# Cached values on TensorE: two batches of four pages in a row every fourth tick, in place of one batch every second tick

## The reference

```python
def diff_attn_sample(q, k_new, v_new, k_past, v_past, lam):
    ...
    s = jnp.concatenate([s_past, jnp.where(causal, s_new, -jnp.inf)], axis=-1)
    p = jax.nn.softmax(s, axis=-1)
    a = (p[:, :, 0] - lam * p[:, :, 1]).astype(v_new.dtype)
    return (jnp.einsum('bhqk,bkhv->bqhv', a[..., :P], v_past)
            + jnp.einsum('bhqk,bkhv->bqhv', a[..., P:], v_new))
```

## Time and profile before

| | us |
|---|---|
| median of 3 timed runs (lowest, highest) | 1393.79 (1392.96, 1394.21) |
| profiled execution, its own time | 1391.86 |
| its span in the profile | 1390.1 |
| PE busy in the span | 1352.7 (97%) |
| DVE / ACT / POOL busy | 900.0 / 579.4 / 397.4 |
| first and last value matmul start (line 3353) | 712.5 and 958.4 |

### The profile page before, as it was taken

One profiled execution on the slowest core, in us unless ns is written; L12 is line 12 of the kernel. 1 busy time (PEld: TensorE's weight loads), 2 busy tenths in 40 slices (PEclk: granted clock), 3 DMA queues, 4 the chain that ended last, 5 costly groups with the idle time before them and its releaser, 6 DMA issues.

```text
span 1390.1 us, 23920 instructions
## 1 busy us (share of the span) xinstructions
PE 1352.7 (97%) x8605; PEld 1124.6 (81%) x8605; DVE 900.0 (65%) x1619; ACT 579.4 (42%) x1075; POOL 397.4 (29%) x395
## 2 busy tenths in 40 slices
PE   9998999999999999999999999999999999999998
PEld 7777877776777767777767766667999999999998
DVE  6479668845648877647657565525376666887785
ACT  7463333315546554623224241314344543435432
POOL 3547424525523544243000000000152102322130
PEclk9999999999999999999999999999999999999999
DMA  9458634434254564577476575874454654232201
GB/s 325 114 183 238 215 136 132 156 118 130 90 159 160 192 231 133 175 253 243 130 267 223 189 250 175 291 229 169 163 193 153 213 204 148 74 122 107 107 32 62
DMA packets 125544, 239.30 MB, mean 172 GB/s; under 512 B 13601, under 2 KB 46658, under 8 KB 125426
## 3 DMA queue, kind: packets, MB, share of 16 engines
q1 hardware_dynamic: 116226, 213.64, 46.4%
q10 hardware_dynamic: 9200, 24.13, 5.2%
HBM read 197.64 MB, written 40.09 MB: 171 GB/s over the span
## 4 chain that ended last, share of the span: by engine, by line
PE 63%; DVE 6%; ACT 2%; issue 2%; DMA 1%; POOL 1%; SPq 1%; ACTq 0%; DVEq 0%; POOLq 0%
PE ps L87 18%; PE ps L89 17%; PE ps L88 17%; PE ps L3353 2%; PE ps L1548 2%; PE ps L1585 1%; PE ps L1367 1%; DMA kr<-in_cache_k 1%; DVE uw_l L2071 1%; ACT uw_h L2065 1%; PE ps L1569 1%; DVE sd L3107 1%; DVE dl L2164 1%; PE ps L1781 1%; DMA vr<-in_cache_v 0%
## 5 line engine op out<-in xcount | busy, mean ns | idle before, releaser
L3118 POOL TENSOR_TENSOR kr<-kr,qb 128x512 f32<-128x512 f32 x128 | 170.6, 1342 | 168.8 <-DMA kr<-in_cache_k 167.6
L87 PE MATMUL ps<-x2hB,uw_h 128*128 128x264 f32 (+1 forms) x512 | 145.2, 284 | 0.7 <-DVE x2lB L2906 0.7
L88 PE MATMUL ps<-x2lB,uw_h 128*128 128x264 f32 (+1 forms) x512 | 144.7, 283 | 0.0
L89 PE MATMUL ps<-x2hB,uw_l 128*128 128x264 f32 (+1 forms) x512 | 144.5, 282 | 0.0
L87 PE MATMUL ps<-part_h,fh 128*128 128x264 f32 (+1 forms) x448 | 127.8, 285 | 0.0
L89 PE MATMUL ps<-part_h,fl 128*128 128x264 f32 (+1 forms) x448 | 127.0, 284 | 0.0
L88 PE MATMUL ps<-part_l,fh 128*128 128x264 f32 (+1 forms) x448 | 126.9, 283 | 0.0
L87 PE MATMUL ps<-uh,dh 128*128 128x512 f32 x256 | 105.8, 413 | 7.2 <-DVE dl L2164 4.9
L2891 DVE TENSOR_TENSOR xt<-xt,ps 128x264 f32<-128x264 f32 (+1 forms) x224 | 87.3, 421 | 35.8 <-PE ps L89 35.6
L3107 DVE TENSOR_REDUCE sd<-kr 128x8 f32<-128x512 f32 x128 | 84.9, 675 | 35.0 <-POOL kr L3118 34.9
L87 PE MATMUL ps<-x2hA,uw_h 128*128 128x512 f32 x256 | 105.6, 412 | 0.0
(11 more groups left out here) (392 smaller groups left out, 3430.3 us busy)
## 6 DMA issues: line engine op xcount, KB each, us to landing
kr<-in_cache_k SPq DMA_DIRECT2D x128, 256.0 KB, 3.4
raw_up<-in_w_up_units SPq DMA_DIRECT2D x64, 512.0 KB, 4.7
vr<-in_cache_v SPq DMA_DIRECT2D x128, 256.0 KB, 3.5
raw_dn<-in_w_down SPq DMA_DIRECT2D x32, 512.0 KB, 6.5
raw_dn<-in_w_down ACTq DMA_DIRECT2D x32, 512.0 KB, 4.9
raw<-in_w_in_units SPq DMA_DIRECT2D x23, 512.0 KB, 6.2
raw_up<-in_w_out_units SPq DMA_DIRECT2D x16, 512.0 KB, 4.3
kept_up_low<-uw_l SPq DMA_DIRECT2D x14, 512.0 KB, 6.6
```

What stands on the lines that cost most here:

```text
L87: pe.matmul(out, lh, rh, start=first and n == 0, stop=False, skip_group_check=onto)
L88: pe.matmul(out, lh, rl, start=False, stop=False, skip_group_check=onto)
L89: ins = pe.matmul(out, ll, rh, start=False, stop=last and n == len(ks) - 1, skip_group_check=onto)
L3118: pool.tensor_tensor(k[:, :], k[:, :], qb[v // PAGES][:, :], ALU.mult).then_inc(k_multiplied, 1)
```

## The change

The body that issues a batch becomes a function, `unit(u)`. The tensor stream calls it for two batches, u - 1 and u, at the tick of each odd batch u, and no more at the ticks of the even ones. The ticks of `total`, of ACT's copies, of DVE's adds and of SP's loads are as they were. SP's waits name the same semaphore values.

```diff
+        def unit(u):
+            b, l = divmod(u, 4)
+            pe.wait_ge(v_in[u % VRING], keys_in[u % VRING] + 64 * (u // VRING + 1))
...
+            if l == 0 and b >= 2:
+                pe.wait_ge(v_added, b)
+            for g in range(4):
+                ins = pe.matmul(ps[32 * g:32 * g + 32, 2 + b % 2, :], sd[:, b, 4 * l:4 * l + 4, :].rearrange("p g h -> p (g h)"),
+                                vring[(4 * u + g) % 8][:, :], start=l == 0, stop=l == 3, tile_position=(0, 32 * g))
+            ins.then_inc(v_used, 1)
+
         for s in range(STEPS):
             u, j = divmod(s - 3, 2)
-            if j == 0 and 0 <= u < VALUE_UNITS:
-                b, l = divmod(u, 4)
-                pe.wait_ge(v_in[u % VRING], keys_in[u % VRING] + 64 * (u // VRING + 1))
...
-                ins.then_inc(v_used, 1)
+            if j == 0 and u % 2 and 0 <= u < VALUE_UNITS:
+                unit(u - 1)
+                unit(u)
             b, j = divmod(s - 11, 8)
             if j == 0 and 0 <= b < NS:
                 total(b)
```

More of the change, by code:

```diff
@@ L3340, in total @@
             ins.then_inc(v_totalled, 1)
+        def unit(u):
+            b, l = divmod(u, 4)
+            pe.wait_ge(v_in[u % VRING], keys_in[u % VRING] + 64 * (u // VRING + 1))
+            if u == 0:
+                pe.wait_ge(sem("exp_made"), 4)
+                pe.wait_ge(sem("coef_made"), 1)
+            if l == 0 and b >= 2:
[4 more added lines that the diff above has]
+            ins.then_inc(v_used, 1)
         for s in range(STEPS):
             u, j = divmod(s - 3, 2)
-            if j == 0 and 0 <= u < VALUE_UNITS:
-                b, l = divmod(u, 4)
-                pe.wait_ge(v_in[u % VRING], keys_in[u % VRING] + 64 * (u // VRING + 1))
[L3347 to L3354, removed]
-                ins.then_inc(v_used, 1)
+            if j == 0 and u % 2 and 0 <= u < VALUE_UNITS:
+                unit(u - 1)
+                unit(u)
             b, j = divmod(s - 11, 8)
```

## The result

| | before | after | ratio (95% interval) |
|---|---|---|---|
| median, us (first comparison) | 1393.26 | 1402.21 (1399.59 to 1404.78) | 1.0059 (1.0046 to 1.0072) |
| median, us (second comparison) | 1394.14 | 1402.71 (1399.33 to 1407.60) | 1.0065 (1.0043 to 1.0087) |
| span of the profiled execution | 1390.1 | 1400.5 | |

The forecast was 1393.9 us, with 1390.7 to 1398.2 as its range. The time lies above the range.

What follows compares the result with a forecast made beforehand. PE, busy 97% of the span, was taken as the bound. Terms -2.9 (stretches), -0.7 (old wait), +0.6 and +0.4 (DVE), +2.7 (page waits) sum to +0.1 us: 1393.9 us forecast, range 1390.7 to 1398.2.

Steps and rivals of the forecast that it cites:

- The stretches: On PE, nine stretches in the batches' matmul shape go, seven stay for `total`; 0.32 us each, 2.9 us saved.
- The check that I named for it: In the profile after, "issue" idle time in front of the value line falls from 10.2 to about 6 us.
- VectorE's stop: Around 830, PE waits 2.6 instead of 1.4 us for DVE's `dl`; moving batch 14 costs 0.32 instead of saving it: +0.64.
- The +0.4 for batch 6: With batch 6 moved, PE reaches the next tiles 1.2 us earlier than DVE's `dl` allows and waits about 0.4 us.
- The page waits: Second batches of pairs (22,23) and (24,25) wait 1.4 and 1.25 us for pages, +2.7 together; thirteen other intervals within 0.3.
- A sign that I had named for being wrong: The prediction is wrong if pairs before 867 wait for pages, a weight load comes late, or the two waits are missing.
- the walk: Fifteen intervals between pairs checked for late page loads, using SP's order and times; called right to about half a microsecond per tight place.
- The two waits that were named: DMA waits inside the pairs at 901 and 914, (22,23) and (24,25): 1.4 and 1.25 us, each over 1 us.
- Rival 2: Serial issue on SP becomes the bound, second batches late first from 867 on; +3.5 to +4.5, time 1398.3 us, chance 0.16.
- Rival 3: A stop of PE lowers its clock; fifteen slow dense intervals are 3.0 us, time 1396.9 us, chance 0.06.
- "Total follows as before": ACT's copy of a finished sequence waits for its fourth, odd batch, and `total` follows as before; no cost was given.
- Loads behind the value loads priced at nothing: Weights, `rowsB` and other loads behind the pages in SP's order issue up to 8.7 us later; none comes late, no cost.

Runs made afterwards that it cites:

- The kernel without loads: Changed kernel, loading only the first eight pages and reusing them for all 32 batches, so no page can be late: ratio 0.9989 to before.
- number read twice: Changed kernel, with each page number read twice from the page table before its DMA: ratio 1.0265 to before.
- early numbers: Changed kernel, with the eight page numbers of a pair read on SP before the wait for the buffer: ratio 0.9993 to before.
- one row of eight: Changed kernel, page numbers read ahead and all eight page loads of a pair issued in one row, before weights and `rowsB`: ratio 0.9977 to before.
- batches 16 and 17 single: Changed kernel, with batches 16 and 17 alone again on their old ticks and all other pairs kept: ratio 1.0080 to before.

## Why the prediction was wrong

- **The stretches: right.** Nine stretches at 0.32 were forecast to go, seven to stay because of `total`. The rest of the account (-1.85) fits with nine. The kernel without loads, and the 2.1 us that came when `total`'s seven did go, fit too. The Trainium skill (TensorEngine Tiling, "Key Properties") states that a change of the tiling mode drains TensorE. The trace agrees, with 0.32 us for each stretch that is really removed; it does not bear out the sixteen that the prediction drew from that sentence alone. The check that I named for it was bad: "issue" in front of the line did not fall from 10.2 to 6. It is 11.8 in the changed kernel and 15.4 in 48 places without page waits. It also counts what stands inside pairs, so it measures no number of stretches; only intervals from start to start do.
- **VectorE's stop: right** for batch 14 in the stop itself (2.64 us); the step was worth 0.64 by the forecast, 0.4 and 0.3 where two profiles differ by it. The +0.4 for batch 6 did not come: in the changed kernel PE reached that place (767.55) without a wait. The prediction had left DVE's `dl` where it was. It came 1.25 us earlier too, counted from the first mark (766.15 - 705.02 against 764.42 - 702.04), and ended 0.18 before PE.
- **The page waits: the step that failed.** "At thirteen of the fifteen intervals ... nothing is late by 0.3." Three of the thirteen were late, by 1.71, 1.17 and 1.48. The term was 2.7 and measured 6.9, which is 4.2 of the 7.4 us by which the sum was short (+0.1 against +7.47). The low clock, which the sum had at nothing, is the other 3.1. A sign that I had named for being wrong came: a pair before 867 that waits. The causes are in SP's rows. Pair (20,21): foreign issues cost 3.0 us of the row of loads, and two stores with the 2.2 us to the next load are among them; the prediction names no stores in any row. Pair (16,17): two issues for the recurrence stand in its row, which with longer steps took 1.75 more than the forecast has for eight loads; the 0.56 that my own step took off the wait for `xt` also shortened the interval from 13.4 to 12.84, and the last page took 4.2 to land, not 3.5. Pair (28,29): the interval and the issue were in order (10.4), and its last page took 5.9, among weights. I had found the walk "right to about half a microsecond per tight place" on one place of the kernel before. It was right to half a microsecond on none of these.
- **The two waits that were named** came with nearly the forecast's size (1.40 and 1.16 for 1.4 and 1.25). For (24,25) the steps are right too: issued at 11.4 for the 11.3 forecast, landed 3.0 later for 3.3. For (22,23) it is luck. PE's own wait inside (20,21), which I did not have, gave its loads 1.2 us more; a later issue and a landing of 7.6 took it back. In the second profile of the same kernel the two waits are 0.47 and 2.58.
- **Rival 2 (SP's issue becomes the bound) was the true one in the main**, and it had 0.16. Its time, 1398.3, is 4.5 above the median of before; without the low clock the stretch grew by 7.47 - 3.1 = 4.4. I had let it start from 867 on; it started at 857. And I made it depend on longer landings everywhere. The median landing stayed 3.5. Three of the five waits came from the late issue, and two needed a long landing of one page on top.
- **Rival 3 (a stop lowers the clock) came as well**, with 3.1 us for the 3.0 forecast, behind the wait at 857 and not behind those forecast for 901 and 914. The match in size is in part luck: 1.8 of it is dense matmuls, the rest slower small ones, which I had not counted. It had 0.06, and I treated it as an alternative to rival 2, not as something that can come with it. The two together, +4.4 and +3.1, are a case that I did not hold.
- **"Total follows as before": wrong by 0.5 us.** Before, the batch ahead of it stood between ACT's copy and `total`.
- **Loads behind the value loads priced at nothing: right.** In the changed kernel no matmul of the stretch waits for a weight.

What stays open is what makes the clock fall. The mean clock of the kernels with page waits of 6 us and more is 0.992 to 0.993 (0.983 with the number read twice), that of the others 0.994 to 0.996. Within the executions of one kernel, 0.001 of clock goes with about 1 us (0.94 in 29 executions of before, 0.7 to 2.1 in the others), so by an estimate from this the changed kernel's lower mean is worth some 3 us. That the waits cause it is likely, and not shown for a single stop.

## What to carry to other kernels

When two uses of a double buffer are put back to back, the loads for the next two come free together and must all be issued in one interval. Add up what the issuing engine does in that interval, register reads, stores and other streams' loads by name, before pricing the gain, and keep the reads of addresses in front of the wait. A wait that is found in one tight place is a warning for all places whose slack is within a microsecond or two: landings of single pages here varied by more than that. And if PE is made to stop, price the clock with the stop.

## What the runs showed of the hardware

- A page number read from a table costs SP 0.57 us (0.52 against 1.09 between two loads; 0.55 when it is read twice).
- Page loads issued faster land later: median 3.5 at 1.09 apart, 4.8 with early numbers. In one row of eight with the weights behind them it is 4.1, less than in the mixed order, while the weights' median rises from 5.8 to 7.6.
- The same stop of PE in the same kernel is followed by a low clock in one execution and not in another. The two profiles of the changed kernel have a stop of 1.96 and of 1.92 for `dl` at the first mark (705.02 and 705.62). Behind the first the granted clock is 0.57, behind the second 1.00:

```profile
705.00:709.00 4.00, 3.98 (x11) 3.14 (x12) 2.50 (x9) 2.21 (x3) 0.00 (x0) 0.57 0.96 346
```
```profile
706.00:710.00 4.00, 4.00 (x19) 3.25 (x18) 2.64 (x8) 2.11 (x3) 0.00 (x0) 1.00 0.95 329
```

- The length of a stop does not decide it either. A stop of 3.36 us was followed by full clock (851.04, batches 16 and 17 single), and one of 1.96 by the low one.

The Trainium skill (TensorE: Matmul & The Clock Gate, "Part 1: The HAM clock gate") says, of the start of a kernel, that the number of slow matmuls varies between runs of one kernel. The traces here show the like behind a stop in the middle: eight slow intervals between dense matmuls from 705.98 on in the first of these two profiles, none there in the second.
